# Rotation of the rope tiles by DVE shuffles instead of matmuls, and another place for the gate projections of a linear attention

## The reference

```
# first block, layer l (latent tokens; context tokens too, without rope)
z = h @ w_in                    # c_q, c_kv, k_r, dq, dk, dv, ga, gb
qn, qr = rms_norm(c_q) @ w_uq ; kn, va = rms_norm(c_kv) @ w_ukv
qr, kr, q1, q2, k1, k2 = axial_rope(...)       # q1, q2 = dq; k1, k2 = dk
o_a = softmax(qn kn + qr kr) va
o_b = (softmax(q1 k1) - lam * softmax(q2 k2)) vb
x = x + gate * merged(o_a, o_b, ga, gb) @ w_out ; x = x + gate * conv_ffn(x)
# second block, layer l
qa, ka, va, qi, ki, wi, qb, kb, vb, rb, gl, uc = rms_norm(x) @ w_in
qa, ka, qi, ki = partial_rope(...)             # first 16 of each 64 dims
keep = top_k(sum_h wi_h * relu(qi_h . ki))     # index attention picks keys
o_a = softmax over keep of qa . ka, times va
o_b = rms_norm(gated_linear_attention(qb, kb, vb, log_sigmoid(gl))) * silu(rb)
o_c = multiscale_pool(uc)
x = x + [o_a, o_b, o_c] @ w_out ; x = x + conv_glu_ffn(rms_norm(x))
# a rope: (x1, x2) -> (x1 cos - x2 sin, x1 sin + x2 cos)
```

## Time and profile before

| | |
|---|---|
| median of 3 runs | 3508.59 us (3506.32 to 3508.79) |
| span of the profiled execution | 3503.3 us |
| PE busy | 3411.7 us, 97% |
| DVE busy | 2092.1 us, 60% |
| ACT busy | 1318.7 us, 38% |
| POOL busy | 122.4 us, 3% |
| weights read by SP's queue | 442 slabs of 512 KB |

### The profile page before, as it was taken

How to read it: one execution, slowest core, us unless ns; L and a number is a source line. 1 busy time by engine, 2 the same in 40 slices (tenths; PEclk the granted TensorE clock), 3 DMA queues, 4 the chain that set the end, 5 groups by cost and what they waited for, 6 DMA issues and landing times.

```text
span 3503.3 us, 45971 instructions
## 1 busy us (share of the span) xinstructions
PE 3411.7 (97%) x18212; PEld 2726.2 (78%) x18212; DVE 2092.1 (60%) x3304; ACT 1318.7 (38%) x2084; POOL 122.4 (3%) x70
## 2 busy tenths in 40 slices
PE   7999999999999999999999999998999999899998
PEld 5866788888888887767777888776888877688886
DVE  5856653465576655445547664696666449756643
ACT  4454443333213324544434333445322234632222
POOL 0000000000000000000000000150000006000000
PEclk9999999999999999999999999999999999999999
DMA  6411111111362231101122233220232332122332
GB/s 260 147 43 43 49 72 55 61 55 60 111 225 90 100 106 59 38 25 43 61 92 84 94 96 105 91 89 20 91 93 93 105 103 79 43 71 92 96 97 95
DMA packets 79221, 300.56 MB, mean 86 GB/s; under 512 B 8784, under 2 KB 8912, under 8 KB 77904
## 3 DMA queue, kind: packets, MB, share of 16 engines
q1 hardware_dynamic: 77760, 291.47, 25.4%
q10 hardware_dynamic: 1296, 6.82, 0.5%
HBM read 296.16 MB, written 2.10 MB: 85 GB/s over the span
## 4 chain that ended last, share of the span: by engine, by line
PE 89%; DVE 7%; ACT 2%; issue 1%; DMA 0%; POOL 0%; SPq 0%; DVEq 0%; ACTq 0%
PE ps L756 25%; PE ps L758 24%; PE ps L757 24%; PE ps L1075 2%; PE ps L1117 1%; PE ps L1141 1%; PE ps L1155 1%; PE ps L1162 1%; PE ps L1132 1%; DVE work L2945 1%; PE ps L1018 1%; DVE top L2944 1%; PE ps L774 1%; PE ps L1020 1%; PE ps L1019 1%; PE ps L811 1%
## 5 line engine op out<-in xcount | busy, mean ns | idle before, releaser
L2201 DVE TENSOR_TENSOR split<-raw,split 128x1024 fp32r<-128x1024 f32 x406 | 497.2, 1225 | 802.3 <-ACT split L1595 801.7
L1595 ACT ACTIVATE split<-raw 128x1024 fp32r<-128x1024 f32 x436 | 460.2, 1056 | 757.6 <-PE ps L758 685.2
L756 PE MATMUL ps<-h,split 128*128 128x512 f32 x1320 | 528.3, 400 | 0.0
L758 PE MATMUL ps<-h,split 128*128 128x512 f32 x1320 | 520.8, 395 | 0.0
L757 PE MATMUL ps<-h,split 128*128 128x512 f32 x1320 | 520.7, 394 | 0.0
L756 PEld LDWEIGHTS ps<-h,split 128*128 128x128 f32 x1320 | 248.7, 188 | 64.9 <-issue 7.4
L756 PE MATMUL ps<-h_hl,split 128*128 128x512 f32 (+1 forms) x752 | 285.0, 379 | 12.0 <-DVE h_hl L2281 8.9
L757 PEld LDWEIGHTS ps<-h,split 128*128 128x128 f32 x1320 | 248.7, 188 | 59.8 <-issue 3.4
L758 PEld LDWEIGHTS ps<-h,split 128*128 128x128 f32 x1320 | 248.6, 188 | 58.0
L758 PE MATMUL ps<-h_hl,split 128*128 128x512 f32 (+1 forms) x752 | 266.7, 355 | 0.0
L757 PE MATMUL ps<-h_hl,split 128*128 128x512 f32 (+1 forms) x752 | 266.3, 354 | 0.0
(11 more groups left out here) (441 smaller groups left out, 6361.6 us busy)
## 6 DMA issues: line engine op xcount, KB each, us to landing
raw<-wstream SPq DMA_DIRECT2D x442, 512.0 KB, 3.5
ada_t<-ada_w SPq DMA_DIRECT2D x80, 512.0 KB, 4.5
first_w<-ada_first SPq DMA_DIRECT2D x4, 2048.0 KB, 24.9
x<-x_in SPq DMA_DIRECT2D x1, 3072.0 KB, 12.9
x<-x_in ACTq DMA_DIRECT2D x1, 3072.0 KB, 10.9
ada_c<-c_in SPq DMA_DIRECT2D x2, 1024.0 KB, 5.2
out<-x SPq DMA_DIRECT2D x8, 256.0 KB, 2.2
par<-params SPq DMA_DIRECT2D x1, 1345.0 KB, 6.1
```

The lines of the kernel that those rows point to most:

```text
L756: nc.tensor.matmul(o, wh, a[0], start=first, stop=False)
L758: return nc.tensor.matmul(o, wl, a[0], start=False, stop=last)
L1595: nc.scalar.activation(split_of(n)[:, 0, :], raw[:, n % RAW_SLOTS, :], copy).then_inc(hi_split, 1)
L2201: nc.vector.tensor_tensor(split_of(n)[:, 1, :], raw[:, n % RAW_SLOTS, :], split_of(n)[:, 0, :].bitcast(F32), ALU.subtract).then_inc(split_ ...
```

## The change

1. The rotations of the first block and of qi0, qi1 and ki become DVE `stream_shuffle` instructions, the first pass of `rope`; the signs move into the sine tables. The 16 rotations of qa and ka a run stay on PE as `perm`. ACT's 28 copies to `rot` go, a rotation weighs 0 in `key_fills`, and the waits on a free `rot` buffer go from ACT to DVE.
2. `in2`: the rope of qi0 comes ahead of kgw's results, idx(1) comes ahead of uc1 and not behind it, and rb0 and rb1 leave `IN2_PLAIN`.
3. `gla`: rb0 is projected ahead of `products(0)` into bank 6, rb1 between the batches into bank 7; both idle matmuls go. DVE multiplies both out of PSUM by the inverse norm, where POOL did; the silu comes at the end of `dsa`.
4. The multiplication of x in layer 0 comes beside the chunks of the output projection. The pooling chunks of `mix` get a buffer of their own.

```diff
+PARTNERS_A = [i ^ (ROPE_A // 4) for i in range(32)]
+PARTNERS_B = [i ^ (DH_B // 4) for i in range(32)]
+PARTNERS_2 = [i ^ (ROT // 2) if i < ROT else i for i in range(32)]
...
-            pieces.append((2.5, (kind, name, g, DC - 1)))
+            pieces.append((0.0, (kind, name, g, DC - 1)))
...
-IN2_INDEX = (plain(("qi", 0), ("qi", 1), "kgw") + [("rot", ("qi", 0), None), ("rot", ("qi", 1), None)]
-             + plain(("uc", 0)) + [("rot", "ki", None), ("turn", "wi", None)])
-IN2_PLAIN = (plain(("uc", 1)) + indexed(1) + plain("qb") + indexed(2) + plain("kb") + indexed(3)
-             + plain(("rb", 0), ("rb", 1)) + [("gate", "z", None)])
-IN2_ROPED = roped([((name, m), LAT, True) for name in ("qa", "ka") for m in range(HEADS * HD // P)])
+IN2_FIRST = plain(("qi", 0), ("qi", 1))
+IN2_INDEX = ([("rot", ("qi", 0), None)] + plain("kgw") + [("rot", ("qi", 1), None), ("rot", "ki", None)]
+             + plain(("uc", 0)) + [("turn", "wi", None)])
+IN2_PLAIN = indexed(1) + plain(("uc", 1), "qb") + indexed(2) + plain("kb") + indexed(3) + [("gate", "z", None)]
+IN2_ROPED = [("perm" if kind == "rot" else kind, name, g) for kind, name, g in
+             roped([((name, m), LAT, True) for name in ("qa", "ka") for m in range(HEADS * HD // P)])]
...
-            def rotate(perm, src, after, bank=None):
-
-                pe.wait_ge(acc_taken, after)
-                o = open_acc(SEQ, bank)
-                nc.tensor.matmul(o, col(perm, 0, P), src, start=True, stop=True).then_inc(acc_ready, 1)
...
+                    elif kind == "perm":
+                        pe.wait_ge(acc_taken, at[name])
+                        src = (qa if name[0] == "qa" else ka)[:, name[1], :]
+                        nc.tensor.matmul(open_acc(SEQ), col("perm_2", 0, P), src, start=True, stop=True).then_inc(acc_ready, 1)
...
-                            rotate(perm(name), src(name), at[name], bank=NORM_BANK)
                             rots.add()
...
+                gemm(open_slab(), 0, DC, own(h2), (0, SEQ), True, bank=6)
+                pe.wait_ge(acc_taken, res.now(back=1))
...
                 products(0)
-                keep_busy(1)
+                gemm(open_slab(), 0, DC, own(h2), (0, SEQ), True, bank=7)
                 pe.wait_ge(att_off, pairs.now() + 1)
                 pe.wait_ge(att_masked, pairs.now() + 1)
                 products(1)
-                keep_busy(1)
                 pairs.add(2)
...
+                    pe.wait_ge(acc_taken, res.now(back=1 - p))
...
                 if kind == "rot":
-                    o = take(SEQ, False, bank)
-                    k = rots.n
                     rots.add()
-                    if l == 0 and name[0] == "dk":
-                        act.wait_ge(rot_done, k)
-                    elif k >= 2:
-                        act.wait_ge(rot_done, k - 1)
-                    bring(rot[l][rot_place(l, name, k)][:, :], o)
...
+                act.wait_ge(acc_taken, res.now())
+                nc.scalar.activation(rb[:, :, :], rb[:, :, :], ACT.Silu).then_inc(silu_done, 1)
...
-            def rope(dst, rotated, cos, sin):
-
+            def rope(dst, rotated, cos, sin, partners=None):
+
+                if partners is not None:
+                    v(nc.vector.stream_shuffle(rotated, dst, partners))
                 v(nc.vector.tensor_tensor(rotated, rotated, sin, ALU.mult))
                 v(nc.vector.tensor_tensor(dst, dst, cos, ALU.mult))
                 return nc.vector.tensor_tensor(dst, dst, rotated, ALU.add)
...
+                dve.wait_ge(acc_taken, landed[name])
+                if l == 0 and kind == "dk":
+                    dve.wait_ge(rot_done, k)
+                elif k >= 2:
+                    dve.wait_ge(rot_done, k - 1)
+                rope(dst, rot[l][rot_place(l, name, k)][:, :], tab[:, 0, :], tab[:, 1, :], partners).then_inc(rot_done, 1)
...
+                            dve.wait_ge(acc_taken, landed["kgw" if name == "ki" else name])
+                            if j >= 2:
+                                dve.wait_ge(rot_done, rots.now() + j - 1)
+                            dst = ki[:, :] if name == "ki" else qi[:, name[1], :]
+                            rope(dst, rot2[j % 2][:, :], cos2[:, :], sin2[:, :], PARTNERS_2).then_inc(rot_done, 1)
...
+                nc.vector.scalar_tensor_tensor(sin2[:, :], sin_t[:, :], col("turn_sign"), rs_in[:, :], ALU.mult, ALU.mult)\
+                    .then_inc(tab_made, 1)
                 dve.wait_ge(tab_made, 2 * (l + 1))
-                if l == 0:
-                    for k in range(DC):
-                        xk = x[:, k, CTX:TOK]
-                        nc.vector.tensor_tensor(xk, xk, rs_x[:, :], ALU.mult)
...
+                    split_low()
+                    res.add()
+                    dve.wait_ge(slab_used, IN2_AT[l] + IN2_SLABS - 1 + p)
+                    nc.vector.tensor_tensor(rb[:, p, :], ps[:, 6 + p, :], rs_in[:, :], ALU.mult).then_inc(acc_taken, 1)
...
+                def scaled(m):
+                    if l == 0 and m < DC:
+                        xm = in_pieces(x[:, m, CTX:TOK])
+                        v(nc.vector.tensor_tensor(xm, xm, rs_x, ALU.mult))
...
-                split_low(next(slabs))
-                pool.wait_ge(acc_taken, result + 4)
-                nc.gpsimd.tensor_tensor(rb[:, :, :], rb[:, :, :], both, ALU.mult).then_inc(rb_scaled, 1)
...
-        for c0 in (2644, 2772, 1860, 1988, 2372, 2500):
+        for c0 in (2644, 2772, 1860, 1988):
+        for m in range(2):
+            slab(rows(w, span(2372 + m * P)))
```

More of the change, by code:

```diff
@@ L995, in project_after @@
                         t0, K, opens, closes, last = weight(name)
-                        if opens and name not in at:
+                        if opens and name not in opened:
                             w = open_slab()
+                        opened.add(name)
                         gemm(w, t0, K, act(name), g, closes and g == last)
-                        at[name] = res.n
-                    else:
-                        rotate(perm(name), src(name), at[name])
             def own_tokens(l, groups):
@@ L1387, in in2 @@
             def in2(l):
-                src = {"qa": qa, "ka": ka, "qi": qi}
                 def projections(events, at=None):
-                    project(events, lambda name: (0, DC, True, True, LAT[-1]), lambda name: own(h2),
-                            lambda name: "perm_2",
-                            lambda name: ki[:, :] if name == "ki" else src[name[0]][:, name[1], :], layer=l, at=at)
+                    project(events, lambda name: (0, DC, True, True, LAT[-1]), lambda name: own(h2), layer=l, at=at)
                 first = res.n
                 raised_products(l == 0)
-                projections(IN2_INDEX[3:], {("qi", 0): first + 1, ("qi", 1): first + 2, "kgw": first + 3})
+                projections([e for e in IN2_INDEX if e[1] != "kgw"], {"kgw": first + 3})
                 projections(IN2_PLAIN)
@@ L1663, in take_spread @@
                 for i, dst in enumerate(dsts):
-                    ins = nc.scalar.activation(dst[:, :], ps[:, ACC_BANKS + i, :], copy)
+                    ins = nc.scalar.activation(dst, in_pieces(ps[:, ACC_BANKS + i, :]), copy)
                 ins.then_inc(rs_ready, 1)
@@ L2041, in projections @@
                             bring(z, take(SEQ, False), ACT.Identity, bias=col(f"b_gate{l}"))
-                        else:
+                        elif kind == "perm":
                             o = take(SEQ, False)
-                            if j >= 2:
-                                act.wait_ge(rot_done, rots.now() + j - 1)
-                            else:
-                                act.wait_ge(tab_made, 2 * (l + 1))
+                            act.wait_ge(rot_done, rots.now() + j - 1)
                             bring(rot2[j % 2][:, :], o)
-                            if beside is not None:
-                                beside(j)
+                            beside(j)
                             j += 1
-                projections(IN2_INDEX[:1], 0)
+                projections(IN2_FIRST[:1], 0)
                 roots(QT)
@@ L2092, in mix_high @@
             def mix_high(k):
-                nc.scalar.activation(mix_hl[k][:, 0, :], mix[:, k, :], copy).then_inc(hi_ready, 1)
+                nc.scalar.activation(mix_hl[k][:, 0, :], mixed_chunk(k), copy).then_inc(hi_ready, 1)
             def gla(l):
                 for c in range(2):
-                    bring(mix[:, 6 + c, :], take(SEQ, False), ACT.Identity, scale=col(f"pool_scale{l}", c))
+                    bring(mix_pool[:, c, :], take(SEQ, False), ACT.Identity, scale=col(f"pool_scale{l}", c))
                 act.wait_ge(acc_taken, res.now())
@@ L2108, in gla @@
                     ins.then_inc(att_off, 1)
-                act.wait_ge(rb_scaled, l + 1)
-                nc.scalar.activation(rb[:, :, :], rb[:, :, :], ACT.Silu).then_inc(silu_done, 1)
             def dsa(l):
@@ L3184, in axial_table @@
```

(3 more changed lines are left out.)

106 lines of the change are left out of this document (51 added, 55 removed).

## The result

The changed kernel takes 3531.35 us (3530.01 to 3532.5, four runs) beside 3507.45 us (3501.81 to 3508.79, four runs) of the kernel before: a ratio of 1.0074, 95% interval 1.0062 to 1.0086. By the medians it is 24 us slower, by the ratio 26, where I had forecast 3504 and a range that ends at 3518.

What follows compares the result with a forecast made beforehand. PE, busy 97%, was taken as the bound. Heads +3.8, attention -9.9 and second block +1.8 gave -4.3 on 3503.3, so 3499.0; with the runs' median 5.3 above the span, 3504 us, range 3488 to 3518.

Steps and rivals of the forecast that it cites:

- Heads: First block's heads, 14 rotations: DVE's chain takes back PE's gain and PE waits longer; +3.8 us (ends -3, +8).
- Attention: First block's attention, 8 dk rotations: PE time and dk waits saved, shuffles covered on DVE; -9.9 us (ends -11, -6).
- The upper end's missing cover: Attention: were DVE's cover gone, PE would wait up to 0.8 us per rope, 6.4 in all.
- Index tiles: Second block: PE waits 5.5 us per layer for ki's rope ahead of the logits (ends 4, 8), plus 1.7 of clock.
- The search's cover: Second block: ACT waits for DVE's decays, with the search 6 us ahead; charged 0.9 us a layer (ends 0, 3).
- gla: Linear attention with the gate projections moved in: idle matmul 1.0 and waits 1.5 us saved per layer.
- layer 0's clock: Linear attention, layer 0: with a dense projection ahead it runs at layer 1's speed; -2.4 us.
- C: Second block, slower: longer index wait, low clock and late slabs at ACT's decays, +8.4 us a layer, 3518; chance 0.17.
- the qa term: Second block, tiles of qa: the charge for ACT waiting on DVE's decays, 0.9 us a layer (ends 0, 3).

Runs made afterwards that it cites:

- e5: e3 with the 14 rotations of the first block's heads (kr, dq, qr) back on PE with ACT's copies; ratio 0.9965, 3493.98 us.
- e10: e9 with the heads' rotations back on PE; ratio 0.9973 to the kernel before.
- e12: e5 with decay exponentials one qa tile later, rb0 projected in in2, rb1 between the batches, att_off copy ahead of one high half; ratio 0.9979.
- e11: e5 with each of dk's eight shuffles issued twice, same result, 5.9 us more on DVE; ratio 0.9965.
- e1: Changed kernel with uc1's projection put back ahead of the index logits; ratio 1.0050, 3521.11 us.
- e2: Changed kernel with both gate projections back in in2, with POOL's multiplication and gla's idle matmuls; ratio 1.0004, 3505.55 us.
- e9: e7 with ACT's exponentials of the decays each one qa tile later; ratio 0.9986.
- e13: Changed kernel with one line altered: ACT's exponentials of the decays one qa tile later; ratio 1.0045.
- e7: e1 with ACT's copy of each linear-attention batch (att_off) ahead of the next slab's high half; ratio 1.0021, 3513.71 us.
- e14: e12 with ACT's other high half behind the att_off copy too; ratio 0.9946, 3484.85 us.
- e4: Changed kernel with five idle matmuls on PE ahead of the first index logit, filling the wait; ratio 1.0057, 3526.97 us.
- e3: Changed kernel with uc1 back ahead of the index logits and both gate projections back in in2; ratio 0.9985, 3500.37 us.

## Why the prediction was wrong

**Heads: right.** I had +3.8 us in two heads in place of the -12 that counting gives. By ACT's high halves at the attention's start the heads cost 2.0 and 2.2, 4.2 in all. The mechanism, a DVE chain that takes what PE gives, is confirmed by e5. The waits ahead of kn add up to 9.9 us (3.2, 1.4, 5.3), split as the forecast said they might be.

**Attention: right, the nearness of the total in part luck.** -9.9 forecast. From the high half at the attention's start to the first one behind dk's last rotation the change gains 5.2 us in layer 0 (183.68 to 349.56 before, 185.14 to 345.85 after) and 4.5 in layer 1 (1453.39 to 1568.13, and 1449.64 to 1559.92): 9.7. In layer 0, 1.6 of it is given back by the slab at 392.88. Farther on the change gains 3.7 more, in a stretch (392.88 to 763.63 before) with no rotation in it: 370.8 us before, 367.0 after, and, with one and the same first block, 366.7 in e5 but 370.8 in e10 and 370.7 in e12. The granted clock in 520 to 535 is 0.73 before and 0.66 in e10 and e12, and 0.89 after and in e5. That part is the clock and not the change. The upper end's missing cover is excluded by e11, in which 2.1 of 5.9 us show.

**Index tiles: right in the trace, but not separate.** The wait was 5.3 (5.5 forecast) in both layers. The clock lost on work behind it was about 1.9 a layer (1.7 forecast): it is 0.50 from 2245 to 2251, but PE works only from 2247.5. What I hadn't seen is that the wait isn't separate: e1 shows 40% of it coming back at qa.

**The search's cover: the first step that failed.** "I charge 0.9 (ends 0, 3)" was the term for ACT behind the decays. It measured 5.1 us of wait and about 2.5 of clock in layer 0. I had used the row (ACT waits 4.11 us) and the shift of the search (6 us earlier), and left out the term on the other side: the two projections, 11.2 us of PE work, had lain between the logits and qa, and three rotations (2.6) ahead of them. Both engines start the second block 7.8 us sooner. Counted from there, PE comes to qa 8.2 sooner (16.0 less 7.8; 13.8 of work gone, and the logits' wait of 5.3 come in), and DVE's distances only 1.0 sooner (8.8 less 7.8), not 6: the logits, with which the search begins, are themselves only 3.0 sooner (2247.50 beside 2258.25, less 7.8), after their own wait. I priced the projections at the place to which they move, and not what they leave uncovered at the old one. e2, e9 and e13 show it, the last with a single line.

**gla: the second step that failed, with the wrong sign.** I took -2.5 a layer for the idle matmul and waits, and -2.4 for layer 0's clock. The batches' wait for att_off went from 0.67 to 2.62, one of 1.68 came ahead of the scores, and the clock went to 0.54 for 15 us, about 5.8 lost on work. My step was that a dense projection covers the copy; it does, if the copy can start. I had not followed ACT's order through `pass_slab`, whose high half waits for a buffer that the covering projection itself holds. e7 and e14 show it, and e12 by accident. Of the 15 us a layer by which the forecast of the second block is off, the qa term makes about 7 and this one most of the rest; the split is an estimate, since the waits and the clock move one another.

**The rivals.** C named ACT at the decays as one of three sources and lay on the right side, but with +8.4 net a layer against the 16 measured, and with its weight on the index wait and POOL: 8 us there, where 5.3 was measured with one collision. I gave it 0.17, and cut the range at half of it.

## What to carry to other kernels

When filler work moves from one wait to another, price both places: how long the other engine's chain is there, and how much work is left beside it once the filler has gone. Then read the in-order queue of each engine that must react (here ACT) for an instruction ahead of the needed one that waits for the filler itself; one line moved (e13) was worth 10 us, one high half moved (e14) 12. An operation handed from the busiest engine to one that is at 60% pays where that engine is idle in the same stretch (dk: about 10 us), and costs where it is full (heads: 4 to 7 us), whatever the averages say.

## What the runs showed that I had not expected

After a wait of 2 to 5 us the granted clock was low (0.54 to 0.57 in the windows above, so mostly the lower level of 1.2 GHz), and with idle matmuls in the wait it stayed at 1.00 (e4). But such a wait isn't needed. In the kernel before it is 0.50 in 528 to 536 with PE busy throughout from 516 on, and in e3 it is 0.50 from 3000 to 3013, where PE's last idle time was 0.78 us at 2996. And its lows don't fall in the same places from run to run: the linear attention's layer 0 has one before, layer 1 has one in e3, and e2, with the same order of work there, has none. I can't say what decides it; in what these runs show, the same first block ends up to 4 us apart, and part of what a wait seems to cost in clock can be such a low.
